# Expert weights used one expert after the other and given back by halves, in a two-block transformer kernel on one core

## The reference

```python
def hierarchical_moe(h, w_router_group, w_router_expert, w_gate, w_up, w_down):
    # 4 groups x 8 experts; every token goes to the best 2 experts of its best group
    ...
    for g in range(G):
        hg = jnp.einsum('td,edf->tef', h, w_gate[g])      # 1024 -> 512 per expert
        hu = jnp.einsum('td,edf->tef', h, w_up[g])
        act = jax.nn.silu(hg) * hu * comb[:, g, :, None]
        y = y + jnp.einsum('tef,efd->td', act, w_down[g]) # 512 -> 1024
    return y
```

## Time and profile before

| what | value |
|---|---|
| median of three runs | 1006.71 us (999.34 to 1006.77) |
| time of the profiled execution | 1010.48 us |
| its span, first to last instruction | 1008.7 us |
| mean granted TensorE clock | 0.987 of full speed |
| PE busy | 957.3 us, 95% |
| expert stage | from about 564 us to the end |
| data read | 307 MB, mean 307 GB/s |

### The profile page before, as it was taken

One profiled execution on the slowest core, in us unless ns is written; L12 is line 12 of the kernel. 1 busy time (PEld: TensorE's weight loads), 2 busy tenths in 40 slices (PEclk: granted clock), 3 DMA queues, 4 the chain that ended last, 5 costly groups with the idle time before them and its releaser, 6 DMA issues.

```text
span 1008.7 us, 15018 instructions
## 1 busy us (share of the span) xinstructions
PE 957.3 (95%) x6185; PEld 665.4 (66%) x6185; DVE 464.8 (46%) x858; ACT 378.6 (38%) x718; POOL 27.4 (3%) x60
## 2 busy tenths in 40 slices
PE   6899999998999999999989899999999999998987
PEld 3798777898999999988988434343434343332433
DVE  2797756576787468667874411212121112110113
ACT  2465546555666356454662512121212111110211
POOL 1000000000000000002121000000000000000000
PEclk9999999998999999999999999999999999999999
DMA  9968833443754554534666699999999999999996
GB/s 387 400 258 301 331 140 142 202 178 115 274 197 167 177 199 168 199 136 167 269 233 251 265 430 428 427 427 428 428 428 426 428 429 427 427 427 429 429 426 267
DMA packets 23397, 309.34 MB, mean 307 GB/s; under 512 B 2592, under 2 KB 3104, under 8 KB 4000
## 3 DMA queue, kind: packets, MB, share of 16 engines
q1 hardware_dynamic: 23184, 307.32, 74.5%
q10 hardware_dynamic: 144, 1.05, 0.3%
HBM read 307.31 MB, written 1.05 MB: 306 GB/s over the span
## 4 chain that ended last, share of the span: by engine, by line
PE 78%; DMA 14%; DVE 5%; ACT 2%; issue 1%; POOL 0%; DVEq 0%; SPq 0%
PE ps L998 75%; DMA work<-experts 4%; DMA ring<-experts 4%; DMA slot<-experts 4%; DVE wl L1640 1%; DMA ring<-dense 1%; DMA early<-dense 1%; PE ps L1567 1%; PE ps L1196 1%; ACT wh L579 0%; PE ps L1509 0%; ACT hH L804 0%; PE ps L1161 0%; DVE xT L2067 0%; ACT wb L593 0%
## 5 line engine op out<-in xcount | busy, mean ns | idle before, releaser
L998 PE MATMUL ps<-hH,wh 128*128 128x256 f32 x704 | 201.0, 285 | 4.0 <-DVE hL L1664 1.9
L1640 DVE TENSOR_TENSOR wl<-ring,wh 128x1024 fp32r<-128x1024 f32 (+1 forms) x136 | 163.9, 1215 | 81.9 <-ACT wh L579 81.6
L998 PE MATMUL ps<-hL,wh 128*128 128x256 f32 x704 | 198.3, 282 | 0.0
L998 PE MATMUL ps<-hH,wl 128*128 128x256 f32 x704 | 198.2, 282 | 0.0
L579 ACT ACTIVATE wh<-ring 128x1024 fp32r<-128x1024 f32 (+1 forms) x136 | 140.6, 1043 | 121.5 <-PE ps L998 95.3
L998 PEld LDWEIGHTS ps<-hH,wh 128*128 128x128 f32 x704 | 133.9, 190 | 6.1 <-issue 3.7
L998 PEld LDWEIGHTS ps<-hH,wl 128*128 128x128 f32 x704 | 135.6, 193 | 0.0
L998 PEld LDWEIGHTS ps<-hL,wh 128*128 128x128 f32 x704 | 133.8, 190 | 0.0
L2336 DVE SCALAR_TENSOR_TENSOR wc<-wc,w_slot,ps 128x512 f32<-128x512 f32 x16 | 12.0, 748 | 220.9 <-PE ps L998 220.9
L998 PE MATMUL ps<-aH,wh 128*128 128x256 f32 x304 | 86.6, 285 | 5.9 <-DVE wb L2192 2.7
L998 PE MATMUL ps<-aL,wh 128*128 128x256 f32 x304 | 85.7, 282 | 0.0
(11 more groups left out here) (349 smaller groups left out, 1415.6 us busy)
## 6 DMA issues: line engine op xcount, KB each, us to landing
ring<-dense SPq DMA_DIRECT2D x39, 2048.0 KB, 8.5
ring<-experts SPq DMA_DIRECT2D x28, 2048.0 KB, 27.9
slot<-experts SPq DMA_DIRECT2D x28, 2048.0 KB, 28.9
work<-experts SPq DMA_DIRECT2D x20, 2048.0 KB, 28.3
early<-experts SPq DMA_DIRECT2D x10, 2048.0 KB, 26.6
wb<-experts SPq DMA_DIRECT2D x9, 2048.0 KB, 25.3
early<-dense SPq DMA_DIRECT2D x4, 2048.0 KB, 8.7
ring<-dense SPq DMA_DIRECT2D x4, 1024.0 KB, 4.7
```

The lines of the kernel that those rows point to most:

```text
L998: return nc.tensor.matmul(o_, l, r, start=start, stop=stop, skip_group_check=True)
L1640: V.tensor_tensor(wl[:, c % CHUNKS, 0:n], src, wh[:, c % CHUNKS, 0:n].bitcast(F32), ALU.subtract)\
```

## The change

There are four edits. In `gate_or_up` and in the down part, the loop over the experts of the pair goes outside the loop over the slices, and `unit_used` is counted up after each expert, so twice for a unit; all who wait for it have their numbers doubled. Units 10 to 15 are loaded in two halves, each as soon as the matching half of the unit before it in that place is done. Gathers 2 and 3 of the first turn move from ahead of unit 0 to behind it, and ScalarE moves them out after its two small exponentials instead of before. The last up unit (93, `LAST_UP`) is loaded in two halves, and TensorE waits for each by itself.

```diff
+HALVED = range(UNITS, UNITS + 6)
+LAST_UP = PER_PASS - 3
...
-            def load_unit(u):
-                if u < PER_PASS - 1:
+            def load_unit(u, used=None):
+                half = UNIT // 2
+                if u in HALVED:
+                    for i in range(2):
+                        sp.wait_ge(S("unit_used"), used + (2 * (u - UNITS) + i + 1))
+                        sp.dma_start(unit(u)[:, half * i:half * i + half], W["experts"][u][:, half * i:half * i + half])\
+                            .then_inc(unit_loaded(u, 0)[0], 16)
+                elif u == LAST_UP:
+                    sp.dma_start(unit(u)[:, 0:half], W["experts"][u][:, 0:half]).then_inc(S(f"slot{TAIL}_loaded"), 16)
+                    sp.dma_start(unit(u)[:, half:UNIT], W["experts"][u][:, half:UNIT]).then_inc(unit_loaded(u, 0)[0], 16)
+                elif u < PER_PASS - 1:
...
                 for u in range(UNITS, PER_PASS):
-                    sp.wait_ge(S("unit_used"), used + (u - UNITS + 1))
-                    load_unit(u)
+                    if u not in HALVED:
+                        sp.wait_ge(S("unit_used"), used + 2 * (u - UNITS + 1))
+                    load_unit(u, used)
...
             with act.Fori(0, n) as p:
-                for i in range(4):
+                for i in range(2):
                     gather_out(p * TURNS, i, FIRST_BANKS[i])
                 act.wait_ge(S("g_shift"), 1)
                 act.wait_ge(S("norm_rstd"), 5)
                 for tt in range(TT):
                     ins = nc.scalar.activation(gexp[:, tt, :], gtmp[:, tt, :], ACT.Exp, scale=rstd[:, tt:tt + 1])
                 ins.then_inc(S("g_exp"), 1)
+                for i in range(2, 4):
+                    gather_out(p * TURNS, i, FIRST_BANKS[i])
...
                     u = PER_PAIR * q + 2 * part + half
-                    pe.wait_ge(*unit_loaded(u, p))
+                    if u == LAST_UP:
+                        pe.wait_ge(S(f"slot{TAIL}_loaded"), p * 16 + (base_loaded[TAIL] + 16))
+                    else:
+                        pe.wait_ge(*unit_loaded(u, p))
                     w = unit(u)
-                    for kk in range(4):
-                        k = 4 * half + kk
-                        if part == 0 and q % 2 == 0 and k % 2 == 0:
-                            pe.wait_ge(S("xg_out"), p * (4 * TURNS) + (2 * q + k // 2 + 1))
-                        for j in range(2):
+                    for j in range(2):
+                        if j and u == LAST_UP:
+                            pe.wait_ge(*unit_loaded(u, p))
+                        for kk in range(4):
+                            k = 4 * half + kk
+                            if part == 0 and q % 2 == 0 and k % 2 == 0 and j == 0:
+                                pe.wait_ge(S("xg_out"), p * (4 * TURNS) + (2 * q + k // 2 + 1))
                             c0 = 64 * (2 * (q % 2) + j)
                             ins = mm(ps[64 * j:64 * j + 64, part, :], xg[:, k, c0:c0 + 64],
                                      w[:, 2048 * j + 512 * kk:2048 * j + 512 * kk + 512], k == 0, k == KD - 1)
-                    ins.then_inc(S("unit_used"), 1)
+                        ins.then_inc(S("unit_used"), 1)
+                    if u == 0:
+                        pe.wait_ge(S("hn_low"), 4)
+                        for i in range(2, 4):
+                            gather(0, i, FIRST_BANKS[i])
...
-                        for k in range(4):
-                            for j in range(2):
+                        for j in range(2):
+                            for k in range(4):
                                 ins = mm(ps[64 * j:64 * j + 64, 3 + hf, :], eactT[:, k, 64 * j:64 * j + 64],
                                          w[:, 2048 * j + 512 * k:2048 * j + 512 * k + 512], k == 0, k == 3)
-                        ins.then_inc(S("unit_used"), 1)
+                            ins.then_inc(S("unit_used"), 1)
```

More of the change, by code:

```diff
@@ L423, in unit_loaded, with landings @@
             else:
-                return S(f"unit{i}_loaded"), passes * (16 * unit_loads[i]) + 16 * (u // UNITS + 1)
-            return S(name), passes * (16 * unit_loads[i]) + (base_loaded[int(name[4])] + 16 * (u // UNITS + 1))
-        unit_loads = [len(range(i, PER_PASS, UNITS)) for i in range(UNITS)]
+                return S(f"unit{i}_loaded"), passes * (16 * unit_loads[i]) + 16 * landings(u)
+            return S(name), passes * (16 * unit_loads[i]) + (base_loaded[int(name[4])] + 16 * landings(u))
+        def landings(u):
+            return len(range(u % UNITS, u + 1, UNITS)) + sum(v % UNITS == u % UNITS for v in HALVED if v <= u)
+        unit_loads = [landings(max(range(i, PER_PASS, UNITS))) for i in range(UNITS)]
         out_v = out.rearrange("(t p) d -> p t d", p=P)
@@ L435, in _ @@
             sp.dma_start(colT[:], W["cols"]).then_inc(S("cols_loaded"), 16)
-            def load_unit(u):
-                if u < PER_PASS - 1:
+            def load_unit(u, used=None):
[9 more added lines that the diff above has]
+                elif u < PER_PASS - 1:
                     sp.dma_start(unit(u), W["experts"][u]).then_inc(unit_loaded(u, 0)[0], 16)
                 else:
-                    half = UNIT // 2
                     sp.dma_start(unit(u)[:, 0:half], W["experts"][u][:, 0:half]).then_inc(unit_loaded(u, 0)[0], 16)
@@ L485, in _ @@
                 with sp.Fori(1, n) as p:
-                    used = p * PER_PASS
+                    used = p * (2 * PER_PASS)
                     sp.wait_ge(S("unit_used"), used)
@@ L960, in _ @@
                     weight_out(pair)
-                    act.wait_ge(S("unit_used"), pair * PER_PAIR + 2)
+                    act.wait_ge(S("unit_used"), pair * (2 * PER_PAIR) + 4)
                     act.wait_ge(S("w_out"), pair + 1)
@@ L979, in _ @@
                         gather_out(next_turn, 1, 7)
-                    act.wait_ge(S("unit_used"), pair * PER_PAIR + 5)
+                    act.wait_ge(S("unit_used"), pair * (2 * PER_PAIR) + 10)
                     nc.scalar.activation(eH[:, 0:512], ps[:, 3, :], ACT.Copy).then_inc(S("e_high"), 1)
@@ L984, in _ @@
                             gather_out(next_turn, 2, 6)
-                        act.wait_ge(S("unit_used"), pair * PER_PAIR + 6)
+                        act.wait_ge(S("unit_used"), pair * (2 * PER_PAIR) + 12)
                         nc.scalar.activation(eH[:, 512:1024], ps[:, 4, :], ACT.Copy).then_inc(S("e_high"), 1)
@@ L990, in _ @@
                 nc.scalar.activation(eH[:, 512:768], ps[:, 4, 0:256], ACT.Copy).then_inc(S("e_high"), 1)
-                act.wait_ge(S("unit_used"), p * PER_PASS + PER_PASS)
+                act.wait_ge(S("unit_used"), p * (2 * PER_PASS) + 2 * PER_PASS)
                 nc.scalar.activation(eH[:, 768:1024], ps[:, 2, 0:256], ACT.Copy).then_inc(S("e_high"), 1)
@@ L1536, in _ @@
                 pe.wait_ge(S("pick_half"), p * (2 * TURNS) + 2)
-                for i in range(4):
-                    if i % 2 == 0:
-                        pe.wait_ge(S("hn_low"), i + 2)
+                pe.wait_ge(S("hn_low"), 2)
+                for i in range(2):
                     gather(0, i, FIRST_BANKS[i])
@@ L1608, in _ @@
                                      w[:, 1024 * j + 256 * k:1024 * j + 256 * k + 256], k == 0, k == 3)
-                    ins.then_inc(S("unit_used" if quarter else "quarter_done"), 1)
+                    ins.then_inc(S("unit_used" if quarter else "quarter_done"), 1 + quarter)
                     if quarter == 0:
@@ L2334, in _ @@
                     dve.wait_ge(S("e_silu"), pair + 1)
-                    dve.wait_ge(S("unit_used"), pair * PER_PAIR + 4)
+                    dve.wait_ge(S("unit_used"), pair * (2 * PER_PAIR) + 8)
                     V.scalar_tensor_tensor(out=eact, in0=sg, scalar=w_slot[:, 0:1], in1=ps[:, 1, :], op0=ALU.mult, op1=ALU.mult)\
```

## The result

The changed kernel takes 1067.77 us (median of five runs, 1066.52 to 1075.73) against 1005.59 us (five runs, 999.34 to 1006.77; the first three of them gave the 1006.71 us of the table ahead). The ratio is 1.064, with a 95% interval of 1.061 to 1.068. It is slower by 6.4%. The forecast was 1127 us, the stated range 1003 to 1140. The time landed within 5 us of rival 2 (a strip holds five, 1063 us). Medians here are of all executions of a kernel; ratios leave out those of a slower state of the chip, at most two of a kernel.

What follows compares the result with a forecast made beforehand. Transfers were taken to bound the kernel's end, and TensorE after the change: 994.7 us of TensorE alone + 134.2 (expert outside) + 0.3 (switches) = 1129.2 us span, plus 1.8 less 3.8, median 1127 us, 12% slower; range 1003 to 1140.

Steps and rivals of the forecast that it cites:

- rival 2: Expert units: a busy strip holds five instructions, B1 starts 4 s after A1; 70.4 us added, median 1063 us; chance 0.07.
- What bounds the kernel: Expert stage: TensorE to about 833 us, then transfers; turns of 53.0 against 58.7 us, so 5.7 us slack a turn.
- the 14.0 us between the two ends: End of span: TensorE never waiting for transfers would end at 994.7 us, 14.0 below the real 1008.7.
- rival 1: Expert units: B1 overtakes all of A, 13 instructions, so not slower; median 1005 us; chance 0.20.
- 2 s a row: Rows of units under rival 1: loss if nine instructions can be overtaken; s is one matmul step, 0.429 us.
- Two strips at a time: Units on TensorE: strips of expert 0 and expert 1 overlap, a unit taking 8 s, 16 s without overlap.
- Edit 1: Expert loop outside in all units: a lone unit 13 s, n in a row 10 (n - 1) + 13; sum 134.2 us.
- a strip that is busy can hold three instructions back: Strip order under the expert-outside loop: B1 (expert 1) goes when A6 (expert 0) starts, 5 s after A1.
- the sign that the prediction named for rival 2: Trace of a unit: B starts nearer to A than 5 s.
- A1: First of the eight matmuls of strip A in a unit; the next unit's A1 was put at 10 s, when B6 starts.
- Edits 2 to 4: Gathers 2 and 3 behind unit 0, units 10 to 15 halved, unit 93 halved: 0.3 us added, otherwise nothing.
- the switches: Around the moved gathers: two more switches between full width and strips, 0.3 us added for both.

Runs made afterwards that it cites:

- three-and-one: The kernel before with three slices of expert 0, three of expert 1, then the last slice of each; 1027.6 us, ratio 1.019.
- two slices: The kernel before with two slices of expert 0, the same two of expert 1, then the other two of each; 1005.15 us, ratio 0.998.
- slice outside: The changed kernel with the slice loop outside the expert loop again, moved gathers and halved loads kept; 1004.89 us, ratio 0.9999.
- order-alone kernel: The kernel before with the expert loop outside the slice loop in all units, no moved gathers or halves; 1067.24 us, ratio 1.061.
- the first experiment: The changed kernel with only the loop order put back, slices outside experts; moved gathers and halved loads stay; 1004.89 us, ratio 0.9999.
- Gate and up only: The kernel before with the expert loop outside in the gate and up units only, 64 of 96 units; 1026.05 us, ratio 1.020.

## Why the prediction was right or wrong, point by point

**What bounds the kernel: half right.** TensorE to 833 us, then transfers, is so. The sentence that an edit costs nearly nothing below 5.7 us a turn is wrong. The slack is the 14.0 us between the two ends, both of which the prediction had worked out. The forecast's own sum used the whole-sum form and was not touched by this. The bound that rival 1 drew with it was touched: "down to nine, the loss of 2 s a row stays below the slack" is wrong, since three-and-one loses just these two steps a row and its stage is 22 us longer. A slip without effect: the start at 834.65 us is that of turn 5, not 4, four turns after turn 1, as the division by four has it.

**Two strips at a time: right.** It decides the sign, and orders that keep it cost nothing (two slices, slice outside).

**Edit 1, "a strip that is busy can hold three instructions back": this step failed.** The rows of before showed three because the old order never asks for more, and I took the smallest number they need as the limit. The limit is five or six: five are passed, seven are not. B is then four steps late, not five, which is the sign that the prediction named for rival 2. Worse for the sum, a row of units then runs at 8 s each, not at 10 s, because the next unit's A1 is reached when A is just done. So each of the three lone units and the two rows of a turn loses four steps once, and the rest of a row is nearly free: 20 s a turn, not 39. That it is a strip that holds, and not the queue as a whole, the rows of before show: with four strips, the load of the fourth passes three instructions of each of the other three, nine in all. The forecast of +134 us of TensorE became 8 x 9.6 = 77 us, and the slack takes 14 of them. That the measured time lies inside the stated range is luck as far as this step goes: the range took in rivals 1 and 2 beside the forecast. The added time was forecast at some 120 us and is 62.

**Rival 2: right in mechanism, 5 us short.** Its turn was 61.6 us and measured 62.6. In a row a unit starts 3.55 us after the last instead of 3.43, and seven such distances a turn make 0.84 of the 1.0 us. An estimate from the weight loads of unit 0 above: the first step of a strip takes 0.49 us (567.73 to 568.22), each later one 0.43, since its first load is not hidden; two strips that start anew in each unit make 2 x 0.06 = 0.12 us. No run tests this by itself.

**Edits 2 to 4: right that they are worth nothing here**, since the order-alone kernel takes as long as the whole change. By the stage they cost 2.2 us (64.8 against 62.6). That fits the prediction's own count: moved gathers make two lone units of the first row, four steps more, 1.7 us, and 0.3 us for the switches. With the old order they gain nothing either, where rival 1 had put 1.7 us. In the changed kernel the first half of unit 10 went out at 571.41 us, 7.3 us after the first gather instead of 9.0, but the queue then stood still for its second half, and again before unit 11. In the first experiment, below it, all of unit 10 went out early, and unit 11 only at 570.12 us, 12.9 us after the first gather instead of 12.5 before (576.07 us):

```profile
571.41 2.10 SPq L447 DMA_DIRECT2D early<-experts  x2
578.92 8.27 SPq L447 DMA_DIRECT2D work<-experts  x4
```
```profile
564.40 0.80 SPq L447 DMA_DIRECT2D early<-experts  x2
570.12 5.20 SPq L447 DMA_DIRECT2D work<-experts  x4
```

**The chances.** 0.62 stood on a lower bound read as a value. The case that came had the smallest chance but one, 0.07. The gap between "at least three" and "three" deserved more.

## What to carry to other kernels

Where matmuls use only part of the columns, the order in which they are issued decides whether the strips overlap. Alternate them within a few instructions, and count what one strip must leave outstanding before the other's first is reached; two float32 calls each in turn were free here, three were not, and four cost 6%. When two resources race through a stage with work buffered ahead, compare their whole sums, not their rates. A limit that the old trace never reaches is a bound from one side: price the next sizes too before giving one of them most of the chance.

## What the runs showed that was not expected

A busy strip of the array holds back five outstanding instructions without stopping the other, and with seven the other stands still (569.07 and 569.50 us in the changed kernel, 570.80 and 571.23 us in three-and-one). Loads and matmuls of the other strip pass them.

The part ahead of the expert stage, the same code in all of these kernels, does not repeat well. The first gather matmul started at 553.03 us in one profiled execution and at 564.92 us in another, while the stages of three kernels that differ by nothing on TensorE that costs time (before, two slices, slice outside) took 445.1, 445.4 and 445.6 us. For changes below 1% in the stage, its own length says more than the total time. Gate and up only, then three and one:

```profile
553.03 0.55 PE L999 MATMUL ps<-pick,aH 128*128 128x256 f32 x1 [2.67 <-DVE pick L2277]
```
```profile
564.92 0.55 PE L999 MATMUL ps<-pick,aH 128*128 128x256 f32 x1 [2.67 <-DVE pick L2276]
```
